# An encoder layer with expert retrieval on one core: 32 bytes of filler, VectorE's dot products first in the slot, and late attention at six pairs per four heads

## The chip, the cores and the metric

The kernel runs on one core of one Trainium2 chip, with float32 data throughout. Its time is the device time of one execution in microseconds; the number that counts is the median of several runs.

## The reference, cut to what matters

One layer over 1024 tokens of width 1024. Every projection, softmax and sum below is computed:

```python
xn = rms_norm(h, norm_mix)
y_r = retention_branch(...); y_s = sgu_branch(...); y_a = window_attention(...)
merged = sigmoid(gate_r) * (y_r @ w_proj_ret) + sigmoid(gate_s) * (y_s @ w_proj_sgu) + sigmoid(gate_a) * (y_a @ w_proj_att)
h = h + merged @ w_out
# PEER: 8 heads choose 16 of 128*128 experts each, per token
gate = softmax(top_s)                      # scores of the 16 chosen
act = gelu(einsum('thkd,td->thk', u_tab[eid], xt))
h = h + einsum('thk,thkd->td', gate * act, v_tab[eid])
h = h + sigmoid(rms_norm(h, norm_ple) @ ple_gate) * (p @ ple_proj)
```

Each token uses 128 experts, each a row of 1024 numbers of u and 1024 of v, 8 KB together. Of 1024 tokens that is 1.07 GB, gathered by index.

## The kernel before, in words

Three stages run one after the other. The first (keys_stage) makes keys, values and states of all eight tiles of 128 tokens, the second (branches_stage) the branches of tiles 0 to 4, and the third (late_stage, TensorE begins it at 458 us) all the rest. It works in **slots**. From slot 34 on (plan.first) a slot holds one **pair**: two expert rows for each token of a tile. There are 512 pairs, 64 for a tile, eight for one of the eight heads of a tile.

For a row, GpSimd issues an indirect DMA into one of eleven row buffers (l_rows, L1425), after the row that was there has been weighed. VectorE multiplies its u half with the token and sums (dot, L2157). ScalarE makes gelu, weight and, for rows that TensorE adds up, a diagonal matrix (weights, L1873, L1877, L1881). The v half is added by VectorE (weigh, L2167, l_acc or l_merged) or by TensorE through the diagonal (weigh, L1641). TENSOR_ROWS divides rows between the two: 4, 5 or 6 of each eight go to TensorE.

Beside the pairs runs everything that prepares later tiles: a planner (class Plan) gives each **job** a slot. Jobs are projections (gate, proj, query and more, whose weights come through a ring of four 1 MB chunks, all_ring and l_ring), transposes, score products, and for tiles 5 to 7 their retention (rq to ryt) and attention (aq to ayt). Tiles are worked in GROUPS (0, 1), (2, 3, 4), (5, 6, 7); group 2 has its gates and merges behind the attention. The order of the work is written out by hand, once per engine, as a loop over slots:

- TensorE, slot s: weigh of pair s - 1 (counted in slots), then the second halves of jobs begun earlier, then the jobs of slot s.
- ScalarE, slot s: its part of the jobs of slot s - 1, exponentials and norms that fall on s, the search's small steps, then weights of the pair of s.
- VectorE, slot s (L2185 to L2218): order.turn, rotations, squares and gates of tiles 5 to 7, scale, normalise, its part of the jobs of slot s - 1 (merge L1975, add_input L1988, mask_scores L2073, scale_values L2092, reciprocal_rms L2098 and more), the two dots of the pair of s, weigh of pair s - 1, finish at a tile's end, output, and the search for coming heads.
- SP loads the ring, scores, inputs and masks, keyed to slots too; ScalarE stores a few tiles.

Late attention (place_attended, L970) works four heads at a time: asc makes the scores of two heads, twice, mask_scores evacuates them and takes the maximum, attention_exponentials (L1794) follows two slots after the second asc, apt transposes the probabilities of two heads, keep_probs (L1801, L1810) copies them in the slot after, apv multiplies with the values, scale_values divides by the sum. All four heads share one buffer of scores (sc) and all pairs of heads share one of turned probabilities (pt), so keep_probs waits for the apv before it:

```python
before = divmod(job.i * (AH // 2) + job.n - 1, AH // 2)
act.wait_ge(pb_done, plan.of["apv", before[0], before[1]].pb[0] + 1)
```

In build_program small constants stand in SBUF ahead of all_ring, all_xt and the tensors of the stages. Their places follow from their order and sizes, each rounded up to 32 B. ident (512 B a partition), eps, col_ple, iota16, col_ret, sink and decays (160 B) take 864 B from address 8320, so that all_ring begins at 9184, all_xt at 25568, and behind them l_rows at 37856 and l_ring at 127968. The first two stages put a col_mix of 32 B at 37856 and the rest of theirs behind it.

The planner's other numbers that the change touches follow from the attention's slots: earliest (L990) for vs, us and yst of group 2, and rate[2] (L1034), which spreads group 2's work over the slots from the last aqt to ends[2].

Of the kernel before, what the change touches and what calls it, by code (L numbers as in the profile page):

```python
# [17 lines left out]
F32 = mybir.dt.float32  # L18
# [5 lines left out]
P = 128  # L24
# [776 lines left out]
def on_tensor(r):  # L801

    return r % 8 in TENSOR_ROWS[r // NSEL] and r != T * NSEL - 1
# [11 lines left out]
class Plan:  # L815
# [154 lines left out]
    def place_attended(self):  # L970

        at = self.of["pgate", PLE_TILES[0][-1], 1].slot + 2
        for i in range(len(BESIDE)):
            job = self.of["aq", i]
            job.head, job.slot = at, at + 1
            at += 3
        base = self.of["aq", 0].slot + 7
        for u in range(2 * len(BESIDE)):
            i, w = u // 2, u % 2 * 2
            if w == 0:  # L980
                self.of["aqt", i].slot = base - 2
            for k, (score, turn, value) in enumerate(((0, 5, 7), (2, 6, 8))):
                self.of["asc", i, w + k].slot = base + score
                self.of["apt", i, w + k].slot = base + turn
                self.of["apv", i, w + k].slot = base + value
            if w:
                self.of["ayt", i].slot = base + 10
            base += 5

    def earliest(self, job):  # L990

# [98 lines left out]
def late_stage(nc, A, R, X):  # L1090
# [3 lines left out]
    with ExitStack() as ctx:  # L1094
# [116 lines left out]
        def pair_of(s):  # L1211

            g = s - plan.first
            return g if 0 <= g < PAIRS else None
# [710 lines left out]
        def _(dve):  # L1925
# [18 lines left out]
            def normalise(g, i):  # L1944

                k = number(g, i)
                dve.wait_ge(std_ready, k + 1)
                order(dve.reciprocal(mv[:, i, 3:4], mv[:, i, 2:3]))
                order(dve.tensor_scalar(vg(i), vg(i), mv[:, i, 0:1], mv[:, i, 3:4], ALU.subtract, ALU.mult))
                dve.wait_ge(ln_in, (g + 1) * 32)  # L1950
                order(tt(vg(i), vg(i), ln_g, ALU.mult))
                tt(vg(i), vg(i), ln_b, ALU.add).then_inc(vn_ready, 1)
                dve.wait_ge(vn_ready, k + 1)
# [36 lines left out]
            def scale(g, i):  # L1990

                k = sum(len(group) for group in GROUPS[:g]) + i
                dve.wait_ge(rms_ready, k + 1)
                order(dve.reciprocal(rms[:, 2:3], rms[:, 1:2]))
                dve.wait_ge(gain_in, 16 if g < 2 else 32)
                dve.scalar_tensor_tensor(out=scaled(g, i), in0=summed(g, i), scalar=rms[:, 2:3], in1=gain[:], op0=ALU.mult, op1=ALU.mult).then_inc(xs_ready, 1)
                dve.wait_ge(xs_ready, k + 1)
# [38 lines left out]
            def gate_retained(i):  # L2036
                y = kept(i)
                dve.wait_ge(ret_rooted, i + 1)
                order(dve.reciprocal(r_rms[:, RH:2 * RH], r_rms[:, RH:2 * RH]))
                freed_pa(dve, plan.of["rg", i].pa[0])  # L2040
                order(tt(by_4(tb), by_4(silu(i)), wide(r_rms[:, RH:2 * RH], RD), ALU.mult))
                tt(y, y, tb, ALU.mult).then_inc(ret_ready, 1)
                dve.wait_ge(ret_ready, i + 1)
# [6 lines left out]
            def square_query(i):  # L2050
                freed_pa(dve, plan.of["aq", i].pa[0])
                order(tt(tb, qa(i), qa(i), ALU.mult))
                dve.tensor_reduce(a_rms[:, i, 0:AH], by_8(tb), AX.X, ALU.add).then_inc(att_squared, 1)
                dve.wait_ge(att_squared, i + 1)

            def rotate_attention(i):

                def finish(ins):
                    ins.then_inc(qa_ready, 1)
                    dve.wait_ge(qa_ready, i + 1)  # L2060

                dve.wait_ge(att_rooted, i + 1)
                order(dve.reciprocal(a_rms[:, i, AH:2 * AH], a_rms[:, i, AH:2 * AH]))
                order(tt(by_8(qa(i)), by_8(qa(i)), wide(a_rms[:, i, AH:2 * AH], AD), ALU.mult))
                order(tt(by_8(qa(i)), by_8(qa(i)), over(a_gain[:], AH), ALU.mult))
                rotate(order, dve, qa(i), qa(i), spins[:, i, 0:AD // 2], spins[:, i, AD // 2:NA], spun, AH, AD // 2, finish)
# [83 lines left out]
            def dot(r):  # L2150

                t, n = r // NSEL, r % TOPK
                if r % NSEL == 0 and K0 <= t < last[0]:
                    dve.wait_ge(xn_in[t % 2], t // 2 * 16)
                dve.wait_ge(row_in[r % SLOTS], (r // SLOTS + 1) * 16)
                u = rows[:, r % SLOTS, 0:D]
                dve.scalar_tensor_tensor(out=u, in0=u, scalar=1.0, in1=xn_of(t), op0=ALU.mult, op1=ALU.mult,  # L2157
                                         accum_out=dots[:, n:n + 1]).then_inc(dot_done, 1)
# [11 lines left out]
            def finish(t):  # L2170

                dve.wait_ge(acc_done, n_dve((t + 1) * NSEL))
                dve.wait_ge(acc2_done, n_pe((t + 1) * NSEL))
                tt(sum_of(t), sum_of(t), acc2[:], ALU.add).then_inc(h2_ready, 1)  # L2174
                dve.wait_ge(h2_ready, t + 1)
# [8 lines left out]
                    scales_at[plan.of["out", g, 1, i].slot + (3 if g else 2 + 2 * i)].append((g, i))  # L2184
            for s in range(plan.n_slots):  # L2185
                order.turn()
                if s in spins_at:
                    rotate_attention(spins_at[s])
                if s in squares_at:
                    square_query(squares_at[s])  # L2190
                if s in gates_at:
                    gate_retained(gates_at[s])
                for g, i in scales_at[s]:
                    scale(g, i)
                for g, i in normed_at[s]:
                    normalise(g, i)
                for job in plan.at[s - 1] if s else ():
                    if job.kind in programs:
                        programs[job.kind](job)
                if pair_of(s) is not None:  # L2200
                    dot(2 * pair_of(s))
                    dot(2 * pair_of(s) + 1)
                g = pair_of(s - 1)
                if g is not None:
                    for r in (2 * g, 2 * g + 1):
                        if not on_tensor(r):
                            weigh(r)
                if g is not None and (2 * g + 2) % NSEL == 0:
                    finish(2 * g // NSEL)
                for t in range(T):  # L2210
                    for half in range(2):
                        if s == plan.of["pgate", t, half].slot + 2:
                            output(t, half)
                for q, part in plan.parts[s]:
                    if part < 2:
                        search_keys(q, part)
                    else:
                        (search_pairs, choose)[part - 2](q)  # L2218
# [7 lines left out]
def build_program(nc, A, X=None):  # L2226
    if X is None:
        X = {n: nc.dram_tensor(f"kept_{n}", s, F32).ap() for n, s in SPILLS.items()}
    with ExitStack() as ctx:
        R = {"semaphores": Semaphores()}  # L2230
        for n, s, d in (("ident", [P, P], F32), ("eps", [P, 1], F32), ("col_ple", [P, DC], F32), ("iota16", [P, TOPK], F32),
                        ("col_ret", [P, RH], F32), ("sink", [P, AH], F32), ("decays", [P, 40], F32)):
            R[n] = ctx.enter_context(nc.sbuf_tensor("all_" + n, s, d))
        R["ring"] = ctx.enter_context(nc.sbuf_tensor("all_ring", [P, 2, CHUNK], F32))
        R["xt"] = ctx.enter_context(nc.sbuf_tensor("all_xt", [P, max(len(group) for group in GROUPS), D], F32))
        with ExitStack() as mixers:
            for n, s in (("col_mix", [P, DC]), ("decay_mask", [P, RH, P]), ("state_f", [P, T + 1, RW]), ("state_b", [P, T + 1, RW]), ("ka_t", [P, T + 2, P]), ("va", [P, T + 2, AKW]),
                         ("w_branches", [P, DC, KEPT * HB])):
                R[n] = mixers.enter_context(nc.sbuf_tensor("mix_" + n, s, F32))
            keys_stage(nc, A, R, X)  # L2240
            R["semaphores"].clear(nc)
            branches_stage(nc, A, R, X)
            R["semaphores"].clear(nc)
        late_stage(nc, A, R, X)
# [87 lines left out]
```

## Time and profile before

| | us |
|---|---|
| median of 3 runs | 3707.91 (3706.53 to 3715.52) |
| the profiled execution's own time | 3710.65 |
| its span, first to last instruction | 3708.9 |
| TensorE / VectorE / ScalarE / GpSimd busy | 3067.4 / 2667.3 / 1392.0 / 1177.5 |
| mean granted TensorE clock | 0.92 |
| bytes moved by DMA | 1288.92 MB, of which 1073.81 by GpSimd's queue |

Busy time counts compute alone. "DMA share" in a table of stretches is the busy share of the 16 DMA engines; packets overlap a little, so it can be above 1. A wait names the engine and line that waited, then what released it. A packet of the queue is one descriptor; the row loads have 128 of 8 KB and 16 short completions each.

### The profile page before, as it was taken

What the parts mean: (1) busy time and instruction counts of PE and PEld (TensorE: products, weight loads), DVE (VectorE), ACT (ScalarE), POOL (GpSimd) and SP (SyncE); (2) the same over time, 40 slices, a digit from 0 to 9 for tenths busy, and PEclk for the clock granted to TensorE, in tenths of its full rate; (3) what the DMA queues carried; (4) which work ended last, traced back from release to release, by engine and by line L of the source; (5) the groups of instructions that cost most, each with busy time, mean ns of one, the idle gap of its engine ahead of it and who ended that gap; (6) DMA issues with size and microseconds to landing.
All of it is one profiled execution on the core that took longest, in us unless ns stands there. A gap on an engine that the chain in (4) does not pass through costs nothing. (4 is left out here: it accounts for less than half of the span.)

```text
span 3708.9 us, 30990 instructions
## 1 busy us (share of the span) xinstructions
PE 3067.4 (83%) x7876; PEld 1410.0 (38%) x7876; DVE 2667.3 (72%) x5261; ACT 1392.0 (38%) x3615; POOL 1177.5 (32%) x1092
## 2 busy tenths in 40 slices
PE   7989899889988897797898988887786677777666
PEld 4545544434433343333443333343232222223222
DVE  4456511678877877888787887877778778778874
ACT  3223211334433433545453443433453344334332
POOL 0000000233433343232243433433445444444442
PEclk9999799989999998898899999999898998889988
DMA  4331144899999999998899999999999999999995
GB/s 158 103 116 42 41 179 162 325 418 419 418 386 378 419 420 418 381 408 316 317 392 418 419 419 419 419 418 417 396 361 416 420 418 419 419 419 410 419 419 240
DMA packets 210625, 1288.92 MB, mean 348 GB/s; under 512 B 24864, under 2 KB 38048, under 8 KB 63904
## 3 DMA queue, kind: packets, MB, share of 16 engines
q0 software_dynamic: 147456, 1073.81, 70.7%
q1 hardware_dynamic: 57680, 202.86, 14.3%
q10 hardware_dynamic: 5328, 10.49, 0.7%
q8 instruction: 55, 0.90, 0.1%
q14 instruction: 106, 0.87, 0.1%
HBM read 1257.31 MB, written 29.75 MB: 347 GB/s over the span
## 5 line engine op out<-in xcount | busy, mean ns | idle before, releaser
L1641 PE MATMUL l_acc<-l_rows,l_diag 128*128 128x512 f32 x2620 | 1407.9, 677 | 558.9 <-ACT l_diag L1881 552.5
L1425 POOL DMA_INDIRECT l_rows<-in_peer_uv,l_at x1024 | 1163.1, 1136 | 1817.7 <-DVE l_acc L2167 1053.8
L1641 PEld LDWEIGHTS l_acc<-l_rows,l_diag 128*128 128x128 f32 x2620 | 527.9, 212 | 1348.6 <-ACT l_diag L1881 798.8
L2157 DVE SCALAR_TENSOR_TENSOR l_rows<-l_rows,l_xn 128x1024 f32<-128x1024 f32 x640 | 766.0, 1223 | 212.0 <-DMA l_rows<-in_peer_uv,l_at 177.0
L2157 DVE SCALAR_TENSOR_TENSOR l_rows<-l_rows,all_xt 128x1024 f32<-128x1024 f32 x384 | 461.5, 1224 | 165.3 <-DMA l_rows<-in_peer_uv,l_at 136.6
L1873 ACT ACTIVATE l_dots<-l_dots 128x2 f32<-128x2 f32 x512 | 104.1, 203 | 1180.2 <-DVE l_rows L2157 1178.5
L2167 DVE SCALAR_TENSOR_TENSOR l_acc<-l_rows,l_wts,l_acc 128x1024 f32<-128x1024 f32 x272 | 349.0, 1283 | 15.6 <-ACT l_wts L1877 15.6
L1877 ACT ACTIVATE l_wts<-l_dots,l_gates 128x1 f32<-128x1 f32 x1024 | 293.6, 287 | 16.8
L1881 ACT ACTIVATE l_diag<-all_ident,l_wts 128x128 f32<-128x128 f32 x655 | 263.0, 402 | 23.1 <-PE l_acc L1641 1.8
L1418 POOL CAST l_at<-l_expert 128x16 uint32<-128x16 f32 x64 | 14.2, 222 | 667.4 <-DVE l_expert L2143 667.2
L1873 ACT ACT_TABLE_LOAD x139 | 178.3, 1283 | 69.5 <-DVE l_rows L2157 68.2
L1456 PE MATMUL l_pa<-all_ring,all_xt 128*128 128x512 f32 x384 | 178.9, 610 | 4.4 <-PEq L77 4.4
L1465 PE MATMUL l_pa<-l_ring,all_xt 128*128 128x512 f32 x392 | 178.5, 598 | 0.0
L1456 PE MATMUL l_pa<-l_ring,all_xt 128*128 128x512 f32 x360 | 163.6, 597 | 1.3 <-ACT all_xt L1726 1.3
L1465 PE MATMUL l_pa<-all_ring,all_xt 128*128 128x512 f32 x352 | 159.3, 595 | 0.0
L2167 DVE SCALAR_TENSOR_TENSOR l_merged<-l_rows,l_wts,l_merged 128x1024 f32<-128x1024 f32 x97 | 124.3, 1281 | 7.9 <-ACT l_wts L1877 7.8
L1456 PEld LDWEIGHTS l_pa<-all_ring,all_xt 128*128 128x128 f32 x384 | 75.4, 199 | 98.3 <-issue 98.3
L1465 PEld LDWEIGHTS l_pa<-l_ring,all_xt 128*128 128x128 f32 x392 | 75.8, 193 | 96.5 <-issue 96.5
L1695 ACT ACTIVATE l_sgk<-l_pa 128x512 f32<-128x512 f32 x48 | 28.7, 597 | 197.1 <-PE l_pa L1465 197.0
L1975 DVE TENSOR_TENSOR l_sgk<-l_pb,l_sgk 128x512 f32<-128x512 f32 x32 | 22.1, 691 | 110.3 <-PE l_pb L123 107.4
L1465 PEld LDWEIGHTS l_pa<-all_ring,all_xt 128*128 128x128 f32 x352 | 67.6, 192 | 85.8 <-issue 85.8
L1456 PEld LDWEIGHTS l_pa<-l_ring,all_xt 128*128 128x128 f32 x360 | 68.1, 193 | 84.3 <-issue 82.5
(351 smaller groups left out, 3426.1 us busy)
## 6 DMA issues: line engine op xcount, KB each, us to landing
l_ring<-in_w_late SPq DMA_DIRECT2D x58, 1024.0 KB
all_ring<-in_w_late SPq DMA_DIRECT2D x56, 1024.0 KB
l_rows<-in_peer_uv,l_at POOLq DMA_INDIRECT x1024
kept_s<-l_yt ACTq DMA_DIRECT2D x31, 256.0 KB
l_s_in<-kept_s SPq DMA_DIRECT2D x62, 128.0 KB
mix_w_branches<-in_w_branches_kept SPq DMA_DIRECT2D x8, 768.0 KB, 4.3
all_xt<-kept_xnt SPq DMA_DIRECT2D x9, 512.0 KB, 21.7
k_x<-in_x SPq DMA_DIRECT2D x8, 512.0 KB, 5.5
```

The costliest lines, as they stand in the source:

```text
L1418: pool.tensor_copy(at[:, c % 2, :], expert[:, c % 3, :]).then_inc(at_ready, 1)
L1425: pool.indirect_dma_start(out=rows[:, r % SLOTS, :], out_offset=None, in_=A["peer_uv"], in_offset=bass.IndirectOffsetOnAxis(ap=at[:, c % 2 ...
L1456: pe.matmul(out, x[:, c * P:(c + 1) * P], wide_chunk(job.chunk, c), start=(c == 0), stop=False)
L1465: last = pe.matmul(out, x[:, c * P:(c + 1) * P], wide_chunk(job.chunk, c), start=False, stop=(c == DC - 1))
L1641: ins = pe.matmul(acc2[:, hs], diag[n_pe(r) % DIAGS][:], rows[:, r % SLOTS, D + half * HB:D + (half + 1) * HB], start=first, stop=last)
L1695: act.activation(sg(job.i), pa[job.pa[0] % 2][:], ACT.Sigmoid).then_inc(pa_free[job.pa[0] % 2], 1)
L1873: act.activation(dots[:, n:n + 2], dots[:, n:n + 2], ACT.Gelu).then_inc(act_done, 1)
L1877: ins = act.mul(wts[:, m:m + 1], dots[:, m:m + 1], gates[:, c % 3, m:m + 1])
L1881: act.mul(diag[n_pe(r) % DIAGS][:], R["ident"][:], wts[:, m:m + 1]).then_inc(diag_ready, 1)
L1975: evacuate(n, tt(part_sum, pb[n % 4][:], sg(job.i), ALU.mult))
L2157: dve.scalar_tensor_tensor(out=u, in0=u, scalar=1.0, in1=xn_of(t), op0=ALU.mult, op1=ALU.mult, accum_out=dots[:, n:n + 1]).then_inc(dot_do ...
L2167: dve.scalar_tensor_tensor(out=sum_of(t), in0=rows[:, r % SLOTS, D:2 * D], scalar=wts[:, n:n + 1], in1=sum_of(t), op0=ALU.mult, op1=ALU.ad ...
```

## The change

- In build_program a tensor all_even of 8 numbers (32 B a partition) is put ahead of all_ring. Nothing reads or writes it.
- In VectorE's loop the two dots of a slot stand right behind order.turn, ahead of the slot's jobs.
- In place_attended four heads take six slots in place of five: scores at 0 and 3 (before 0 and 2), transposes at 6 and 8 (5 and 6), values at 8 and 10 (7 and 8), the transpose of the finished tile at 12 (10).

```diff
--- before.py
+++ after.py
@@ -979,13 +979,13 @@
             i, w = u // 2, u % 2 * 2
             if w == 0:
                 self.of["aqt", i].slot = base - 2
-            for k, (score, turn, value) in enumerate(((0, 5, 7), (2, 6, 8))):
+            for k, (score, turn, value) in enumerate(((0, 6, 8), (3, 8, 10))):
                 self.of["asc", i, w + k].slot = base + score
                 self.of["apt", i, w + k].slot = base + turn
                 self.of["apv", i, w + k].slot = base + value
             if w:
-                self.of["ayt", i].slot = base + 10
-            base += 5
+                self.of["ayt", i].slot = base + 12
+            base += 6
 
     def earliest(self, job):
 
@@ -2184,6 +2184,9 @@
                     scales_at[plan.of["out", g, 1, i].slot + (3 if g else 2 + 2 * i)].append((g, i))
             for s in range(plan.n_slots):
                 order.turn()
+                if pair_of(s) is not None:
+                    dot(2 * pair_of(s))
+                    dot(2 * pair_of(s) + 1)
                 if s in spins_at:
                     rotate_attention(spins_at[s])
                 if s in squares_at:
@@ -2197,9 +2200,6 @@
                 for job in plan.at[s - 1] if s else ():
                     if job.kind in programs:
                         programs[job.kind](job)
-                if pair_of(s) is not None:
-                    dot(2 * pair_of(s))
-                    dot(2 * pair_of(s) + 1)
                 g = pair_of(s - 1)
                 if g is not None:
                     for r in (2 * g, 2 * g + 1):
@@ -2231,6 +2231,7 @@
         for n, s, d in (("ident", [P, P], F32), ("eps", [P, 1], F32), ("col_ple", [P, DC], F32), ("iota16", [P, TOPK], F32),
                         ("col_ret", [P, RH], F32), ("sink", [P, AH], F32), ("decays", [P, 40], F32)):
             R[n] = ctx.enter_context(nc.sbuf_tensor("all_" + n, s, d))
+        R["even"] = ctx.enter_context(nc.sbuf_tensor("all_even", [P, 8], F32))
         R["ring"] = ctx.enter_context(nc.sbuf_tensor("all_ring", [P, 2, CHUNK], F32))
         R["xt"] = ctx.enter_context(nc.sbuf_tensor("all_xt", [P, max(len(group) for group in GROUPS), D], F32))
         with ExitStack() as mixers:
```

## Rows read from the trace of the kernel before

**Rows 1.** The profile's page: busy shares, and GB/s moved in 40 slices

```profile
PE 3067.4 (83%) x7876; PEld 1410.0 (38%) x7876; DVE 2667.3 (72%) x5261; ACT 1392.0 (38%) x3615; POOL 1177.5 (32%) x1092
GB/s 158 103 116 42 41 179 162 325 418 419 418 386 378 419 420 418 381 408 316 317 392 418 419 419 419 419 418 417 396 361 416 420 418 419 419 419 410 419 419 240
```

**Rows 2.** The page's chain of work that ended last

```profile
DMA 8%; PE 1%; issue 1%; DVE 1%; ACT 0%; POOL 0%; DVEq 0%; POOLq 0%
```

**Rows 3.** Stretches: us; busy PE, PEld, DVE, ACT, POOL; clock, DMA share, GB/s

```profile
680.00:1060.00 380.00, 340.28 (x829) 152.88 (x830) 297.15 (x559) 156.29 (x375) 133.22 (x124) 0.94 1.01 417
1060.00:1200.00 140.00, 123.04 (x288) 54.57 (x287) 104.25 (x203) 48.35 (x125) 42.71 (x42) 0.94 0.94 373
1200.00:1540.00 340.00, 290.90 (x825) 139.56 (x826) 269.70 (x503) 139.57 (x360) 119.09 (x112) 0.94 1.02 418
1540.00:1600.00 60.00, 46.42 (x125) 21.37 (x123) 49.42 (x99) 25.67 (x65) 19.41 (x19) 0.86 0.92 351
1660.00:1880.00 220.00, 180.35 (x558) 90.24 (x557) 177.50 (x358) 113.66 (x281) 67.64 (x66) 0.91 0.84 321
1880.00:2640.00 760.00, 650.34 (x1561) 287.52 (x1559) 602.57 (x1185) 300.53 (x817) 299.59 (x277) 0.93 1.01 418
2640.00:2780.00 140.00, 122.06 (x272) 52.65 (x272) 105.99 (x214) 74.72 (x182) 61.00 (x53) 0.92 0.92 366
2780.00:3660.00 880.00, 607.94 (x1132) 235.75 (x1132) 701.15 (x1421) 326.81 (x1007) 399.20 (x366) 0.88 1.01 417
```

**Rows 4.** Waits in 1660 to 1880 us: who for whom, total, times, longest

```profile
DVE l_yt L2073 <- PE l_pb L1589: 13.2, 5, 8.3
DVE l_ht L2092 <- PE l_pb L1606: 13.2, 4, 5.0
DVE l_bn L1939 <- ACT l_merged L1672: 5.8, 1, 5.8
ACT l_gain L1810 <- PE l_pb L1606: 31.0, 5, 9.7
PE l_acc L1641 <- ACT l_diag L1881: 36.7, 18, 7.6
POOL l_rows L1425 <- DVE l_acc L2167: 115.9, 23, 11.9
```

**Rows 5.** VectorE's waits in 1060 to 1200, 1540 to 1600, 2640 to 2780

```profile
DVE l_sgk L1975 <- PE l_pb L123: 13.6, 2, 7.7
DVE l_merged L1988 <- PE l_pb L1465: 11.5, 3, 6.5
...
DVE l_yt L2048 <- PE l_pb L1551: 6.7, 1, 6.7
DVE l_prms L2098 <- ACT l_prms L1830: 1.5, 1, 1.5
...
DVE l_prms L2098 <- ACT l_prms L1830: 19.4, 3, 7.3
```

**Rows 6.** VectorE's waits for rows in 2050 to 2300 us

```profile
DVE l_rows L2157 <- DMA l_rows<-in_peer_uv,l_at: 30.2, 24, 3.8
```

**Rows 7.** Groups by line: the dot products of 640 rows

```profile
L2157 DVE SCALAR_TENSOR_TENSOR l_rows<-l_rows,l_xn 128x1024 f32<-128x1024 f32 x640 | 766.0, 1223 | 212.0 <-DMA l_rows<-in_peer_uv,l_at 177.0
```

**Rows 8.** DMA in 11.5 to 17.5, 527.2 to 529.8, 2900 to 3100 us

```profile
DMA packets 1215, 2.46 MB, mean 409 GB/s; under 512 B 16, under 2 KB 16, under 8 KB 1215
q1 hardware_dynamic: 1215, 2.46, 105.1%
...
DMA packets 151, 1.11 MB, mean 425 GB/s; under 512 B 16, under 2 KB 16, under 8 KB 16
q1 hardware_dynamic: 151, 1.11, 100.6%
...
DMA packets 12352, 83.80 MB, mean 419 GB/s; under 512 B 1373, under 2 KB 2013, under 8 KB 2269
```

**Rows 9.** Timeline of VectorE at the first rows: start, us, what

```profile
680.14 1.23 DVE L2157 SCALAR_TENSOR_TENSOR l_rows<-l_rows,l_xn 128x1024 f32<-128x1024 f32 x1 [3.79 <-DMA l_rows<-in_peer_uv,l_at]
```

## The prediction

> **What bounds the kernel now.** First the page's slices [rows 1]: from the ninth on, the sixteen DMA engines move 416 to 420 GB/s in most slices, while TensorE is busy 83% and VectorE 72% of the span. The chain that ended last [rows 2] names the landing of expert rows with 8%, everything else with 1% or less. The reader should see a transfer-bound kernel with an even ceiling, so that the question is where it falls below the ceiling. The table of stretches [rows 3] answers: 417 to 418 GB/s in the four long ones, less in four short ones. With 419 as the ceiling (the mean of the fullest stretch, [rows 8]), the transfer time lost is W x (419 - rate) / 419: 140 x 46/419 = 15 us in 1060 to 1200, 60 x 68/419 = 10 us in 1540 to 1600, 220 x 98/419 = 52 us in 1660 to 1880 (the late attention, pairs 183 to 213), 140 x 53/419 = 18 us in 2640 to 2780 (the gates of tiles 2 to 4). Sum: 95 us. As the bytes do not change, the change can win only from these 95 us, or by raising the ceiling.
>
> Why the ceiling is missed in the attention stands in its waits [rows 4]. GpSimd, which issues the rows, waits 116 us for VectorE to free a row: transfers run dry because rows are held, not because issuing is slow. VectorE is busy 177.5 of 220 us [rows 3]; of its 42.5 us idle, 26.4 are waits for TensorE's attention scores (L2073) and values (L2092). TensorE waits 36.7 us for the diagonals of ScalarE, and ScalarE waits 31.0 us at L1810, five times and up to 9.7 us, for TensorE's values (L1606). That is a ring: the probabilities of the second pair of heads are copied in the same slot in which TensorE makes the values of the first, ScalarE's row weights stand behind that copy, and TensorE's values stand behind the weights of the slot before.
>
> **The change part by part.** *The filler.* Tensors are laid out in order at multiples of 32 B, so 32 B more move the first ring from 9184 (17 x 512 + 480) to 9216 (18 x 512), and the rows from 37856 to 37888 (74 x 512); both now begin 224 B past a multiple of 256. The tensors of the first two stages, aligned now behind their 32 B col_mix, go 32 B off. The trace has both kinds [rows 8]. Loads of weights in 2 KB packets to an aligned tile (11.5 to 17.5 us) keep the engines full at 409 GB/s, 16 x 2048 / 409 = 80.1 ns a packet. Ring loads in 8 KB packets, misaligned (527.2 to 529.8 us), reach 425 GB/s with their completions, 308.4 ns. The difference, 228.3 ns for 6144 B, is 26.9 B/ns, and leaves 80.1 - 76.1 = 4 ns fixed for the aligned packet and 308.4 - 304.5 = 4 ns for the misaligned one. No room is left for a cost of the start address, so I take 0. Bounds: a misaligned row packet could be what separates rows (419) from that ring load (425): (425 - 419) / 425 = 1.4% of the 2360 us in the four full stretches [rows 3], 33 us gained; nothing excludes the same in the other sense for the tiles that go off, but there the slices show 41 to 179 GB/s [rows 1], so it is hidden under TensorE, with 2 us as bound if the saturated 6 us load lost a third.
>
> The row speaks against any gain here. The Trainium skill (DMA: Bandwidth & Descriptors, section How a descriptor splits into AXI transactions) speaks for one: a transfer that begins off a 256 B boundary also pays for the bytes below its start, here 7 beats of 32 B on 256, or 2.7%. As an estimate by that page 2.7% of about 2850 us would be 76 us and the sum would end near 3590; by that rule the misaligned load could not have reached 425 with its completions, and the trace does not agree.
>
> *Dot products first.* In each slot VectorE now does the two dots (2 x 1.22 us, [rows 7]) before the rotations, scalings and evacuations of the slot before; then the weighing, as now. Nothing is added and no DMA is issued by the moved code; SP's and GpSimd's lists keep their order, and only the semaphores of VectorE's jobs rise later, those of the dots earlier. The length of the cycle changes. Now dots(s) stand behind jobs(s-1), which need TensorE's slot s-1, which needs ScalarE's weights(s-2), which need dots(s-2): one pass of the ring serves two slots. Afterwards only dots(s+1) stand behind it, so that it serves three. Each wait of VectorE for a job is covered by 2.45 us more work.
> - 1060 to 1200: waits of 13.6 and 11.5 us for TensorE in 5 pieces [rows 5]; 5 x 2.45 = 12 us covered, 8 taken, since TensorE is busy 123 of 140 and 15 is all that can be won.
> - 1540 to 1600: one wait of 6.7 and one of 1.5 us; 2.45 + 1.5 = 4 taken.
> - 2640 to 2780: VectorE waits three times, 19.4 us, for ScalarE's root of the tile (L2098); 3 x 2.45 = 7 covered, 5 taken, because ScalarE's own chain of that job is as long as before.
>
> In the full stretches the cost is a later job: dots wait for rows there, 30.2 us in 24 pieces in 250 us [rows 6], 1.3 us each, and each job is now behind that and 2.45 us of dots. Cover: rows are asked for 5 pairs ahead, TensorE is idle 110 of 760 us in 1880 to 2640. I put 5 us for it all, with bounds of 0 and the rival below. In the opening the first dots wait 3.8 us for their landing [rows 9] before jobs that then are later by that, on a VectorE with nothing urgent: 0, at most 4.
>
> *Six pairs per four heads.* Attention takes 35 slots to its last turn now (base to base + 35), 42 then; scores at 0 and 3 of 6 in place of 0 and 2 of 5, transposes 6 and 8, values 8 and 10. The second copy of probabilities (slot 9) meets values made in slot 8, so the 31.0 us of L1810 lose their reason, and with them most of the diagonals' 36.7. What then bounds is VectorE's own work: 177.5 busy and some 9 us of gaps between its instructions (42.5 less 26.4, 5.8 for L1939 and a little) give 187 in place of 220. The seven slots more are ordinary ones, where VectorE idles 157 of 760 us [rows 3], about 1.2 us a pair: up to 8 us further relief, of which the longer chain of exponentials (now behind the later masks) takes part. Transfers alone need 220 x 321/419 = 169. I take a gain of 30, bounds 10 (only L1810's share that falls on a row release) and 52. Group 2 behind it gets 125 slots for what had 129, TensorE's work there 3% denser: 20 us of work into 110 us of idle time, 0, and its last score comes 3 slots later, long before the tiles need it. What is late next is VectorE itself.
>
> Sum: 30 + 8 + 4 + 5 - 5 - 0 = 42 us off. The profiled execution took 3710.65 us (span 3708.9), so it would be 3669; it stands 2.7 us above the median of 3707.91, for which the forecast is 3666.
>
> **The rivals.** (1) *The start address counts after all*, worth 33 us by rows: 3666 - 33 = 3633, and down to 3590 by the rule named above. Against it the packet times [rows 8]; for it only that rows run at 419 and not 425, which their issue by GpSimd can explain. Chance 0.10. (2) *The wait moves and little comes of it*: with VectorE free in the attention, ScalarE's exponentials and TensorE, busy 180 of 220 us, keep the rows held; a gain of 10 less 5: 3703. Chance 0.15. (3) *Slower: jobs behind the row wait.* In 1880 to 2640 each of group 2's 27 evacuations (18 merges, 6 outputs, 3 mixings) is later by the dots and, at worst, the longest row wait, 2.45 + 3.8 = 6.25 us; if TensorE stood still each time, 27 x 6.25 = 169 us against its 110 us idle: 59 lost, 42 won, 3725. It decides from 110/27 = 4.1 us a job on. For it: TensorE at 86% is the next engine to be full. Against: four buffers of PSUM and jobs placed two or more slots apart. Chance 0.14. (4) That the change does not do what it says touches the filler alone, whose effect I count as nothing; the two reorderings change instructions directly.
>
> **How the numbers follow.** A measurement of this kernel can tell about 0.3%, 11 us, from no change. The forecast's case has 0.61, rival 1 0.10, together 0.71 faster; rival 2 lies around the edge, 0.01 of it beyond: faster 0.72, same 0.14, slower 0.14. The likeliest case alone spans 3629 (79 of the 95 us) to 3696. The range takes in all 95 us (3613) and reaches up past the middle of no change to 3710; left out are the far part of rival 1 (0.04) and rival 3 with its neighbours (0.14).
>
> **What would show it.** Right: about 390 GB/s or more from 1660 to 1920, L1810's waits for TensorE gone, L2073's and L2092's under 10 us together, GpSimd's wait for L2167 there halved; L2098's waits shorter by 2 us each. 419 GB/s where it was full shows the filler idle, 425 rival 1. Wrong: TensorE waiting for pb buffers or for L1975 in 1880 to 2640, and below 415 GB/s there (rival 3); the attention still at 330 GB/s with ScalarE waiting at L1798 (rival 2).

## The result, and the profile after

The changed kernel takes 3619.57 us (median of 4 runs, 3616.38 to 3624.38), the kernel before 3709.52 us in the same comparison (4 runs, 3706.53 to 3715.52). The ratio is 0.9757, 95% interval 0.974 to 0.9774. So 90 us are gone, 2.4%, more than twice the 42 of the forecast; the time is inside the range, near its lower end. The profiled execution has a span of 3614.6 us.

The page of the changed kernel, its busy line, its GB/s in 40 slices and its chain, against [rows 1, 2]:

```profile
PE 3027.8 (84%) x7876; PEld 1398.3 (39%) x7876; DVE 2668.0 (74%) x5261; ACT 1389.0 (38%) x3612; POOL 1207.9 (33%) x1092
GB/s 154 97 129 43 27 172 169 287 425 426 426 426 426 424 425 407 410 405 351 397 400 426 426 427 426 427 425 425 420 409 424 427 422 421 422 419 401 427 424 240
DMA 3%; PE 1%; issue 1%; DVE 0%; ACT 0%; POOL 0%; DVEq 0%; POOLq 0%
```

Two things are to be seen. The dips are shallower: the attention's slices stood at 316 and 317, now the lowest is 351, and those at 386, 378 and 381 are gone. And the ceiling itself has risen: full slices stood at 418 to 420 GB/s and now stand at 425 to 427. Counts and busy times are almost those of before: nothing became cheaper on an engine.

The stretches of the changed kernel (us; busy PE, PEld, DVE, ACT, POOL; granted clock, DMA share, GB/s), against [rows 3]:

```profile
680.00:1060.00 380.00, 348.69 (x864) 156.74 (x865) 305.43 (x578) 162.73 (x390) 139.96 (x129) 0.96 1.01 425
1060.00:1200.00 140.00, 123.21 (x294) 55.30 (x293) 117.77 (x215) 59.16 (x145) 55.09 (x48) 0.94 1.01 426
1200.00:1540.00 340.00, 289.26 (x842) 142.24 (x843) 276.16 (x534) 136.40 (x362) 118.44 (x111) 0.92 1.00 414
1540.00:1600.00 60.00, 55.68 (x125) 24.08 (x124) 51.81 (x98) 25.51 (x63) 27.61 (x22) 0.95 1.00 408
1660.00:1880.00 220.00, 193.95 (x627) 97.68 (x628) 198.92 (x410) 116.79 (x307) 89.81 (x80) 0.92 0.95 380
1900.00:2600.00 700.00, 604.39 (x1455) 268.64 (x1454) 560.26 (x1104) 286.68 (x772) 288.75 (x261) 0.95 1.01 426
2640.00:2780.00 140.00, 114.78 (x247) 47.49 (x246) 118.80 (x248) 66.43 (x184) 63.89 (x59) 0.94 1.01 415
2780.00:3500.00 720.00, 499.12 (x948) 193.73 (x947) 583.11 (x1203) 272.03 (x831) 329.14 (x303) 0.89 1.01 421
```

Stretches are cut by the clock, not by work, so a row of after holds somewhat later work than its row of before; the steps are read in the rates, not in the busy times. 680 to 1060 and 1900 to 2600 were full before (417 and, within [rows 3], 418) and are full now, at 425 and 426. Of the four short stretches one is full (426), two are nearly so (408 and 415) and the attention is mended in part (380). Two full stretches have lost a little of their fullness: 414 in 1200 to 1540 and 421 in 2780 to 3500, under a ceiling of 426.

The waits of the changed kernel in 1660 to 1880 us (who for whom: us, times, longest), against [rows 4]:

```profile
DVE l_yt L2073 <- PE l_pb L1589: 8.5, 4, 3.3
DVE l_ht L2092 <- PE l_pb L1606: 2.2, 1, 2.2
ACT l_gain L1810 <- PE l_pb L1597: 28.6, 9, 6.7
PE l_acc L1641 <- ACT l_diag L1881: 27.6, 9, 6.7
POOL l_rows L1425 <- DVE l_acc L2167: 110.6, 26, 8.8
```

VectorE's waits for TensorE's scores and values went from 26.4 to 10.7 us. ScalarE's wait at L1810 for the values (L1606) is gone, but ScalarE now stands 28.6 us at the same line for the transposes (L1597; 6.5 us before). GpSimd's wait for VectorE to free a row is nearly what it was, while it issues 74 rows in that time and not 62: 115.9 / 62 = 1.9 us a row before, 110.6 / 74 = 1.5 now.

VectorE's waits of the changed kernel in 1060 to 1200, in 2640 to 2780 and in 2050 to 2300 us, against [rows 5, 6]:

```profile
DVE l_merged L1988 <- PE l_pb L1465: 7.5, 4, 4.1
DVE l_sgk L1975 <- PE l_pb L123: 3.3, 1, 3.3
...
DVE l_prms L2098 <- ACT l_prms L1830: 3.3, 1, 3.3
...
DVE l_rows L2157 <- DMA l_rows<-in_peer_uv,l_at: 26.2, 18, 3.1
```

### The profile page after: what moved, and what is told of

Same layout as the page of the kernel before. It is cut to its first block and busy times, and to the rows that moved or that the text cites. A ratio compares the mean times of both kernels' runs of the same rounds, so it can differ in the third digit from the quotient of the medians.

```text
span 3614.6 us, 30882 instructions
## 1 busy us (share of the span) xinstructions
PE 3027.8 (84%) x7876; PEld 1398.3 (39%) x7876; DVE 2668.0 (74%) x5261; ACT 1389.0 (38%) x3612; POOL 1207.9 (33%) x1092
## 5 line engine op out<-in xcount | busy, mean ns | idle before, releaser
L1641 PE MATMUL l_acc<-l_rows,l_diag 128*128 128x512 f32 x2620 | 1383.4, 668 | 501.2 <-ACT l_diag L1881 494.6
L1425 POOL DMA_INDIRECT l_rows<-in_peer_uv,l_at x1024 | 1191.7, 1164 | 1694.6 <-DVE l_acc L2167 952.3
L2167 DVE SCALAR_TENSOR_TENSOR l_acc<-l_rows,l_wts,l_acc 128x1024 f32<-128x1024 f32 x272 | 349.3, 1284 | 7.2 <-ACT l_wts L1877 3.8
L2167 DVE SCALAR_TENSOR_TENSOR l_merged<-l_rows,l_wts,l_merged 128x1024 f32<-128x1024 f32 x97 | 124.3, 1282 | 4.2 <-ACT l_wts L1877 4.0
L522 PE MATMUL b_p<-mix_w_branches,b_xnt 128*128 128x512 f32 x192 | 92.1, 632 | 0.0
```

Of the source, the lines that this page charges most:

```text
L522: last = pe.matmul(out[:], x[:, c, :], R["w_branches"][:, c, column:column + HB], start=(c == 0), stop=(c == DC - 1))
L1425: pool.indirect_dma_start(out=rows[:, r % SLOTS, :], out_offset=None, in_=A["peer_uv"], in_offset=bass.IndirectOffsetOnAxis(ap=at[:, c % 2 ...
L1641: ins = pe.matmul(acc2[:, hs], diag[n_pe(r) % DIAGS][:], rows[:, r % SLOTS, D + half * HB:D + (half + 1) * HB], start=first, stop=last)
L2167: dve.scalar_tensor_tensor(out=sum_of(t), in0=rows[:, r % SLOTS, D:2 * D], scalar=wts[:, n:n + 1], in1=sum_of(t), op0=ALU.mult, op1=ALU.ad ...
```

## The experiments

The forecast said that the filler does nothing and that the two reorderings give 42 us. So the three parts were first run one by one, then the filler was taken from the whole. Times below are medians. The kernel before was measured beside each group of experiments: 3710.13 us beside the first four (11 runs), 3710.7 beside the three starts and the first of "both aligned", 3709.61 beside the last three.

**The filler alone.**

```diff
+        R["even"] = ctx.enter_context(nc.sbuf_tensor("all_even", [P, 8], F32))
         R["ring"] = ctx.enter_context(nc.sbuf_tensor("all_ring", [P, 2, CHUNK], F32))
```

> The 32 B filler alone on the kernel before. Theory A (start address): misaligned packets cost some 4 to 6 ns each once transfers have been continuous for 10 to 15 us, so the ceiling goes from 419 to 426 GB/s for the whole row stage, 1.6% of about 2850 us: 46 us less, 3664, with the slow attention stretch still there at about 325 GB/s. Rival O (order): the higher rate in the changed kernel came with the dots' new place, which spreads VectorE's accesses; then the filler alone is worth under 8 us and the full stretches stay at 419.

3675.91 us (3670.4 to 3680.29), ratio 0.9905 [0.9888, 0.9921]: 34 us gained by 32 B that hold nothing. Two of its stretches, columns as above:

```profile
1660.00:1880.00 220.00, 178.65 (x574) 90.35 (x575) 175.97 (x358) 113.97 (x281) 68.50 (x66) 0.92 0.84 322
1900.00:2600.00 700.00, 611.53 (x1460) 270.76 (x1459) 561.56 (x1093) 281.76 (x763) 289.19 (x260) 0.94 1.01 426
```

The attention stays at its 322, but what was full at 419 is now full at 426. By this one run the step "so I take 0" has fallen. The stretch from 680 to 1060, full before, gained nothing by itself: it moved 417 GB/s with and without the filler.

**The dot products first, alone.**

```diff
                 order.turn()
+                if pair_of(s) is not None:
+                    dot(2 * pair_of(s))
+                    dot(2 * pair_of(s) + 1)
...
-                if pair_of(s) is not None:
-                    dot(2 * pair_of(s))
-                    dot(2 * pair_of(s) + 1)
```

> Only the dots moved ahead, no filler, attention at five slots. Theory A: ceiling stays at 419 GB/s; the short stretches recover 25 to 35 of the 95 us lost, 3675 to 3685, and most of the attention's loss (ScalarE at L1810) remains. Rival O: ceiling 424 or more, 3640 or less.

3670.8 us (3668.04 to 3673.93), ratio 0.9892 [0.9875, 0.9909]: 39 us. Its stretches, and its waits in 1660 to 1880 us:

```profile
1060.00:1200.00 140.00, 124.65 (x297) 55.95 (x295) 115.37 (x212) 55.64 (x138) 52.68 (x46) 0.96 1.01 419
1200.00:1540.00 340.00, 289.38 (x840) 141.62 (x840) 270.79 (x516) 132.95 (x352) 118.61 (x109) 0.92 1.01 411
1660.00:1880.00 220.00, 192.84 (x629) 98.45 (x628) 193.30 (x387) 117.05 (x300) 82.33 (x76) 0.95 0.91 358
...
ACT l_gain L1810 <- PE l_pb L1606: 41.0, 6, 11.2
PE l_acc L1641 <- ACT l_diag L1881: 19.0, 12, 4.7
DVE l_ht L2092 <- PE l_pb L1606: 6.8, 2, 4.0
DVE l_yt L2073 <- PE l_pb L1589: 2.8, 3, 1.7
```

Here is the row that corrects the picture of the attention. ScalarE's wait at L1810 for the values grew, from 31.0 to 41.0 us, and yet TensorE waits only 19.0 us for the diagonals (36.7 before) and the rate rose from 321 to 358. What fell is VectorE's waiting for scores and values, from 26.4 to 9.6 us. That wait of ScalarE was long and cost little.

**Six pairs per four heads, alone.**

```diff
-            for k, (score, turn, value) in enumerate(((0, 5, 7), (2, 6, 8))):
+            for k, (score, turn, value) in enumerate(((0, 6, 8), (3, 8, 10))):
...
-                self.of["ayt", i].slot = base + 10
-            base += 5
+                self.of["ayt", i].slot = base + 12
+            base += 6
```

> Only the six slots per four heads. If ScalarE's wait at L1810 for TensorE's values is what holds the attention, it disappears and 20 to 30 us come off, 3680 to 3690, with the stretches before 1660 us as in the kernel before. If VectorE's waits for TensorE hold it (then it is the dots' place that matters), under 10 us.

3701.45 us (3690.91 to 3706.33, 8 runs), ratio 0.9972 [0.996, 0.9983]: 9 us. Its attention, and its waits in 1660 to 1880 us:

```profile
1660.00:1880.00 220.00, 176.27 (x528) 85.71 (x528) 176.29 (x356) 105.57 (x264) 65.90 (x67) 0.88 0.87 334
...
PE l_acc L1641 <- ACT l_diag L1881: 41.4, 16, 8.3
DVE l_yt L2073 <- PE l_pb L1589: 27.5, 5, 8.7
ACT l_gain L1810 <- PE l_pb L1597: 25.6, 7, 6.3
```

The wait for the values is gone as foretold, and TensorE waits for the diagonals more than before (41.4 against 36.7 us), VectorE for TensorE 27.5 at L2073 alone (13.2 before). The spacing breaks the link that the forecast named, and the wait moves on, as rival 2 had it. A likely reason, not tested by itself, is that VectorE still stands in its jobs before it comes to the dots.

**Both reorderings, no filler.**

```diff
-        R["even"] = ctx.enter_context(nc.sbuf_tensor("all_even", [P, 8], F32))
```

> The changed kernel without its filler. Theory A: 46 us slower than the changed kernel, 3665, ceiling 419 GB/s. Rival O: within 8 us of 3620. If the parts add, this gain and that of the filler alone sum to 90 us.

3661.95 us (3660.69 to 3666.58), ratio 0.9867 [0.9851, 0.9884]: 48 us, which is 39 + 9 of the two alone. Its stretches:

```profile
1060.00:1200.00 140.00, 128.03 (x306) 57.61 (x305) 117.65 (x222) 56.87 (x142) 51.76 (x46) 0.96 1.01 419
1200.00:1540.00 340.00, 288.54 (x823) 140.44 (x822) 266.20 (x507) 132.13 (x346) 122.31 (x112) 0.91 1.01 411
1540.00:1600.00 60.00, 47.40 (x125) 21.76 (x124) 53.66 (x108) 25.73 (x66) 23.08 (x19) 0.91 0.96 375
1660.00:1880.00 220.00, 185.30 (x604) 92.90 (x603) 200.23 (x400) 119.58 (x311) 86.59 (x77) 0.92 0.94 374
1900.00:2600.00 700.00, 601.29 (x1439) 265.15 (x1437) 551.76 (x1076) 279.24 (x748) 283.82 (x255) 0.95 1.01 419
2640.00:2780.00 140.00, 118.66 (x271) 50.37 (x270) 117.43 (x234) 74.14 (x197) 63.41 (x57) 0.96 1.00 407
2780.00:3500.00 720.00, 492.28 (x935) 192.13 (x933) 573.41 (x1176) 267.99 (x817) 311.77 (x298) 0.89 1.01 413
```

This kernel is the one that the forecast of 3666 describes. Without the filler the ceiling is back at 419.

**Which boundary, and which rule.** Three kernels differ from the changed one in the filler's size alone, so that rings and rows begin on a multiple of 256 but not of 512, 32 B past a multiple of 256, and 128 B past one (before: 224 B past). The filler has 288, 64 and 160 B for that; each cut is against the changed kernel.

```diff
-        R["even"] = ctx.enter_context(nc.sbuf_tensor("all_even", [P, 8], F32))
+        R["even"] = ctx.enter_context(nc.sbuf_tensor("all_even", [P, 72], F32))
```

> The changed kernel with 288 B of filler, so that rows and weights begin at an odd multiple of 256 B. Theory A1: the cost comes from a start off a 256 B boundary; then this is as fast as the changed kernel, 3620, with row stretches at 426 GB/s. Rival A2: 512 B is the unit; then as without filler, 3662, 419 GB/s.

3619.76 us (3617.5 to 3625.85), ratio 0.9765 [0.9748, 0.9782]: the changed kernel's time. A multiple of 256 is enough.

```diff
-        R["even"] = ctx.enter_context(nc.sbuf_tensor("all_even", [P, 8], F32))
+        R["even"] = ctx.enter_context(nc.sbuf_tensor("all_even", [P, 16], F32))
```

> The changed kernel with 64 B of filler: rows and weights begin 32 B past a multiple of 512. If bytes below the start are paid for (the rule of beats), 1 beat of 32 B in 256 here in place of 7: 0.4% of 2850 us, at most 11 us over 3620, 3626 to 3631. If it is one more transaction for a packet whatever the offset, the same as without filler: 3660, 419 GB/s.

3661.51 us (3657.61 to 3664.06), ratio 0.9875 [0.9858, 0.9891]: the time without a filler (3661.95). 32 B past a boundary cost as much as 224.

```diff
-        R["even"] = ctx.enter_context(nc.sbuf_tensor("all_even", [P, 8], F32))
+        R["even"] = ctx.enter_context(nc.sbuf_tensor("all_even", [P, 40], F32))
```

> The changed kernel with 160 B of filler: rows and weights begin 128 B past a multiple of 256. By beats below the start 4 of the 7, 24 us over 3620: 3644, about 422 GB/s. By one more transaction for a packet: 3660, 419 GB/s.

3652.12 us (3650.06 to 3655.36), ratio 0.985 [0.9834, 0.9866]: it costs 32 of the 42 us. DMA in 2000 to 2200 us of the kernel before and of these three, in this order (before, 256, 32, 128):

```profile
DMA packets 12006, 83.81 MB, mean 419 GB/s; under 512 B 1331, under 2 KB 1843, under 8 KB 1843
...
DMA packets 12328, 85.29 MB, mean 426 GB/s; under 512 B 1360, under 2 KB 2000, under 8 KB 2000
...
DMA packets 12009, 83.85 MB, mean 419 GB/s; under 512 B 1329, under 2 KB 1841, under 8 KB 1841
...
DMA packets 12049, 84.14 MB, mean 421 GB/s; under 512 B 1334, under 2 KB 1846, under 8 KB 1846
```

Single packets say the same. Counted from the packet records of the expert rows (8 KB each) in 2800 to 3200 us:

```
kernel              start past 256   mean ns   at 309 ns   at 313 ns
before              224 B            315.3      8%         50%
both reorderings    224 B            317.4     23%         42%
start 32 past        32 B            317.0     20%         44%
start 128 past      128 B            315.9     44%          7%
start 256             0 B            312.3     98%          0%
changed kernel        0 B            311.8     99%          0%
```

A packet to an unaligned start takes 313 ns most often, in place of 309, whether it is 32 or 224 B past; in the mean it is 5 to 6 ns more (317.0 and 317.4 against 311.8 and 312.3). At 128 B 44% of the packets stay at 309 and 53% lie between 311 and 321 ns, and the cost in time is three quarters of the others'; no theory here foretold that, and it stays open.

**What else goes unaligned, and where the gain sits.** The filler puts the tensors of the first two stages 32 B off. This kernel aligns them as well:

```diff
-            for n, s in (("col_mix", [P, DC]), ("decay_mask", [P, RH, P]), ...
-                         ("w_branches", [P, DC, KEPT * HB])):
+            for n, s in (("decay_mask", [P, RH, P]), ...
+                         ("w_branches", [P, DC, KEPT * HB]), ("col_mix", [P, DC]), ("pad", [P, 120])):
```

> The changed kernel with the first two stages' tensors at multiples of 512 B as well (their 32 B col_mix goes to the end, with 480 B behind it). The 2 KB weight packets of the first 20 us, 88 ns in the changed kernel, should be 84 again as in the kernel before. Theory: the first key products start 0.5 us earlier, everything else there is hidden under TensorE; 0 to 2 us off 3620. Rival: the early stages pay in every transfer, 3 to 6 us off.

3613.81 us (3613.44 to 3620.3), ratio 0.975 [0.9732, 0.9767], 6 us under the changed kernel with intervals that overlap. The stretches showed no place for a gain, so it was measured a second time, together with a kernel in which only the rows and what stands behind them are aligned: no filler ahead of the rings, 32 B ahead of the rows in its place.

```diff
-        R["even"] = ctx.enter_context(nc.sbuf_tensor("all_even", [P, 8], F32))
...
+        pad = sb("pad", [P, 8])
         rows = sb("rows", [P, SLOTS, 2 * D])
```

> The changed kernel without its filler ahead of the rings; in its place 32 B stand directly ahead of the expert rows. So rows and the late rings begin on a multiple of 256 B, the first rings, the x tiles and the late tensors of the first stages stay as they were before the change (the tensors of the first two stages aligned, the first rings 224 B past a multiple). Theory (the cost of an unaligned start falls on the row packets, because they keep the transfers full for long): all of the filler's gain is back, 3613 to 3622 us, rows at 425 to 427 GB/s from 1900 to 2600 us and 8 KB packets of 309 ns. Rival (the rings' alignment carries part of it): 3630 to 3650 us.

3620.36 us (3615.94 to 3621.57), ratio 0.9765 [0.9749, 0.9782]: the changed kernel's time. Rows at a multiple of 256, with the two ring chunks (l_ring) behind them, are all of the gain; the first two ring chunks (all_ring) and the x tiles count for nothing that can be measured. Rows and l_ring were not taken apart.

> The kernel of e8_both_aligned a second time, in more rounds: everything that is loaded begins on a multiple of 256 B, the tensors of the first stages too. It was 5.8 us under the changed kernel there, with intervals that overlapped. Theory (early transfers are hidden under TensorE, so nothing but a little of the first weight load can be won): within 2 us of the rows-only kernel of the same call. Rival (the first load's slower packets are on the path): 3 to 8 us under it.

3620.92 us (3618.52 to 3625.42), ratio 0.9767 [0.975, 0.9785]. The 6 us were not there a second time, on another chip and beside the rows-only kernel: nothing that repeats is gained by aligning the early stages.

The rows-only kernel gives the cleanest look at the first load of weights (2 KB packets), which it has aligned and the changed kernel 32 B off. Stretches of 2 us of that load, first of the changed kernel, then of rows only:

```profile
11.50:13.50 2.00, 0.85 (x4) 0.88 (x5) 0.92 (x2) 0.00 (x0) 0.00 (x0) 1.00 1.05 410
13.50:15.50 2.00, 1.09 (x6) 0.69 (x4) 0.82 (x1) 0.00 (x0) 0.00 (x0) 1.00 1.04 392
15.50:17.50 2.00, 0.80 (x1) 0.50 (x2) 0.92 (x4) 0.90 (x1) 0.00 (x0) 1.00 1.05 389
```

```profile
11.50:13.50 2.00, 0.83 (x4) 0.86 (x5) 0.92 (x2) 0.00 (x0) 0.00 (x0) 1.00 1.05 410
13.50:15.50 2.00, 1.11 (x6) 0.71 (x4) 0.80 (x1) 0.00 (x0) 0.00 (x0) 1.00 1.05 408
15.50:17.50 2.00, 0.87 (x1) 0.50 (x2) 0.94 (x4) 0.88 (x1) 0.00 (x0) 1.00 1.05 408
```

Both start at 410. Only after about 2 us does the unaligned load fall to 392 and 389. The forecast's witness for "no cost" was a ring load, of which this is the course in the kernel before:

```profile
526.00:528.00 2.00, 2.00 (x6) 0.85 (x5) 0.00 (x0) 0.00 (x0) 0.00 (x0) 1.00 0.77 299
528.00:530.00 2.00, 2.00 (x6) 0.95 (x5) 0.69 (x1) 0.00 (x0) 0.00 (x0) 1.00 0.99 418
530.00:532.00 2.00, 2.00 (x6) 0.85 (x5) 0.22 (x1) 0.00 (x0) 0.00 (x0) 1.00 0.67 283
```

It was full for some 4 us (527 to 531), longer than those 2 us, so the first load alone doesn't explain why it showed no cost. The 8 KB packets themselves do. In the kernel before, where all of them go to unaligned starts, 98% of the row packets from 680 to 684 us took 309 ns, 69% from 684 to 688 and 5% from 688 to 692, with transfers at 0.96 or more of full from 674 us on. With 8 KB packets the cost came some ten microseconds into full transfers, and this ring load, whose packets took 309 ns from 528 to its end, was over by then. Why the cost comes late at all, and later for 8 KB than for 2 KB, no run here shows.

**The spacing once more, with the filler and the early dots.**

```diff
-            for k, (score, turn, value) in enumerate(((0, 6, 8), (3, 8, 10))):
+            for k, (score, turn, value) in enumerate(((0, 5, 7), (2, 6, 8))):
...
-                self.of["ayt", i].slot = base + 12
-            base += 6
+                self.of["ayt", i].slot = base + 10
+            base += 5
```

> The changed kernel with five pairs per four heads again: filler and early dots stay. Without the filler the spacing was worth 3670.8 - 3661.95 = 8.9 us on top of the early dots. Theory (the parts are linked only by the share of the time in which transfers are full): the spacing is worth a little more with faster transfers, 9 to 16 us, so 3629 to 3636 us, with the attention from 1660 to 1880 us near 363 to 370 GB/s. Rival (the spacing's worth is already in the early dots, and 8.9 was noise): within 4 us of the changed kernel, 3620 to 3624 us.

3631.89 us (3624.87 to 3634.16), ratio 0.9797 [0.9781, 0.9814]; attention and gates:

```profile
1660.00:1880.00 220.00, 196.05 (x646) 99.95 (x645) 194.76 (x402) 114.67 (x294) 86.65 (x78) 0.97 0.92 369
2640.00:2780.00 140.00, 115.17 (x240) 48.01 (x238) 115.38 (x242) 64.48 (x174) 71.37 (x60) 0.90 0.99 398
```

So the spacing is worth 12 us on top of the two others. With all runs side by side, each part alone and on top of others:

```
part       alone   on top of
filler     34.2    42.4 (both reorderings)
dots       39.3    39.5 (spacing), 44.0 (filler)
spacing     8.7     8.9 (dots), 12.3 (filler and dots)
```

The 82 us of the parts alone make 90 together. Stretches cut by the clock hold different work in each kernel, so here is the same split by work. Counted from the issue times of the rows (L1425): when the first is issued, how long the kernel takes from the issue of one pair to that of another, and what is left behind the last pair, in us of the profiled executions.

```
pairs           before  filler   dots  spacing  both, no filler  changed
first issue      668.1   668.3   663.9   667.6        672.4       667.3
0 to 96          609.6   609.6   600.7   606.2        600.3       590.6
96 to 160        431.8   426.1   423.3   432.4        424.5       417.4
160 to 256       589.1   580.4   570.8   582.4        560.1       554.5
256 to 320       370.9   364.9   371.6   371.6        369.3       363.0
320 to 511       989.0   971.9   987.6   984.4        986.4       970.2
to the end        50.6    52.9    51.5    52.3         51.9        51.7
```

The filler alone gains nothing in pairs 0 to 96, and 9.7 us there on top of the reorderings (600.3 to 590.6). That is where its 34 us become 42: faster transfers pay only where nothing else holds the rows back, and the early dots have taken other waits out of those pairs. The first issue moves by up to 8.5 us between these kernels (663.9 to 672.4), by no part in particular; that was not run down.

## Why the prediction was wrong, and where it was right

**The filler, the step that failed.** The forecast took two packet times, aligned 2 KB at 80.1 ns and misaligned 8 KB at 308.4 ns, solved them for 4 ns fixed in both kinds, and wrote "No room is left for a cost of the start address, so I take 0". The runs show 34 us alone and 42 on top. Three faults lie in the step. First, the working could not have found a cost: with one rate drawn through two packet times, the time left over is the same 4 ns at both by construction, and any price of an unaligned start would have gone into the rate of 26.9 B/ns. Second, the misaligned figure came from a burst of 2.6 us, before such a load shows its cost, as the packet times above say. And third, the row that spoke against it stood in the same group [rows 8]: the rows' own 419 over 200 us, which was set aside as "their issue by GpSimd". With the filler the same gathers run at 426. Rival 1 had 33 us, from a ceiling of 425 in place of 419 over the four full stretches, and that is the 34 of the filler alone, in part by luck: one of the four, 680 to 1060, gained nothing. On top of the reorderings it was 42, and the difference sits in pairs 0 to 96. From both reorderings to the changed kernel the rate rises by 7 GB/s in 680 to 1060, in 1060 to 1200 and in 1900 to 2600 (the last alone is 700 x 7/419 = 12 us), by 8 in 2780 to 3500, by 6 in the attention and by 3 in 1200 to 1540.

**What the Trainium skill's rule was right and wrong in.** The forecast said of the Trainium skill (DMA: Bandwidth & Descriptors, section How a descriptor splits into AXI transactions) that the trace does not agree. In direction it agrees: a start off a 256 B boundary costs, and one at a multiple of 256 doesn't. In size it does not. Paying for the bytes below the start would make 224 B cost 7 beats and 32 B one. (The section words this for bytes that are fetched; the filler moves the written side, in SBUF, so the runs speak of that side alone.) As an estimate by that page of the Trainium skill these are 76 us, as the forecast had it, and a seventh of it, 11 us; measured were 42 and 42. What fits rows of both sizes is a fixed price of a packet: 16 x 2048 B at 410 and 389 GB/s are 79.9 and 84.2 ns, 4.3 ns more; 8 KB packets go from 309 to 313 ns at their most common, 4 ns more, and by 5 to 6 ns in the mean. That this is one more transaction per packet is an inference; no run isolates it, and 128 B, with its spread, doesn't quite follow it.

**The reorderings, right in sum.** Their sum was 42, measured 48 (3666 forecast, 3661.95 measured with both and no filler; the profiled executions are only 44 apart, 3710.65 and 3666.58, the latter being the slowest of its four). Taken apart as W x (rate gained) / 419, from [rows 3] to that kernel's stretches:

```
stretch        GB/s        gives   forecast
1060 to 1200   373 to 419   15.4      8
1540 to 1600   351 to 375    3.4      4
1660 to 1880   321 to 374   27.8     30
2640 to 2780   366 to 407   13.7      5
1200 to 1540   418 to 411   -5.7     } -5
2780 to 3500   417 to 413   -6.9     }
sum                         47.7     42
```

The rates flatter the short stretches and blame the long ones behind them. By work, from the table of pairs, both reorderings gain 9.3 us in pairs 0 to 96, 7.3 in 96 to 160, 29.0 in 160 to 256, 1.6 in 256 to 320 and 2.6 in 320 to 511, and the start and the end lose 4.3 and 1.3: together 44, the distance of the two profiled executions.

- *1060 to 1200.* The forecast took 8 us. All 15 that could be won came by the clock, but pairs 64 to 80 take 10 us less (112.0 to 102.0) and pairs 80 to 96 then 10.6 more (96.3 to 106.9). Transfers are full in those (418 GB/s from 1166 to 1266 us), so they carry bytes there that the kernel before had moved earlier. What is kept up to pair 96 is 9.3 us, part of it from 680 to 1060, where the forecast had none.
- *2640 to 2780.* L2098 runs three times, and in the changed kernel two of these come before 2640 us, so the one wait of 3.3 us above is not the whole. All three, in 2560 to 2780, for the kernel before, dots alone, both without filler, and the changed kernel:

```profile
DVE l_prms L2098 <- ACT l_prms L1830: 19.4, 3, 7.3
DVE l_prms L2098 <- ACT l_prms L1830: 12.5, 3, 5.0
DVE l_prms L2098 <- ACT l_prms L1830: 6.8, 3, 3.6
DVE l_prms L2098 <- ACT l_prms L1830: 8.0, 3, 3.6
```

The dots alone shorten each by 2.3 us, as forecast; the rest came with the spacing, by a way that was not run down. In time little of it is kept, 2.6 us from pair 320 to the last.
- *The attention's 30 us* was right in size and wrong in cause, so its size is luck. (It lies at pairs 149 to 179; the 183 to 213 of the forecast are slots.) It was put on the spacing, by way of the wait at L1810. The dots alone give 220 x 37/419 = 19 us there with that wait longer than before; the spacing alone 220 x 13/419 = 7 with that wait gone. By work it is the same: 18, 7 and 29 us for dots, spacing and both in pairs 160 to 256. That the wait that decided is VectorE's own, at L2073 and L2092, fits the dots (26.4 to 9.6 us) but is not shown: with the spacing alone these two waits grew to 31.2 us and the rate still rose, to 334. "L1810's waits for TensorE gone" was a wrong sign too: they now go to L1597. Two more signs were narrowly missed, 387 GB/s from 1660 to 1920 where 390 was asked, and 10.7 us at L2073 and L2092 where it was under 10.
- *GpSimd's wait for L2167 halved* did not come (115.9 to 110.6). There are eleven row buffers whatever the speed; the wait per row is what fell, from 1.9 to 1.5 us.
- *Later jobs, -5.* In 1880 to 2640, where the forecast looked, there is no loss: 418 GB/s with both reorderings, and waits for rows in 2050 to 2300 are 26.2 us in the changed kernel, 30.2 before. Of rival 3's signs one wait of TensorE for L1975 is seen, 3.4 us. By rates 13 us are lost in 1200 to 1540 and in 2780 to 3500, but by work no block of pairs in the table is slower than before, so much of that can be the same bytes moved at another time. One new dip is plain, 345 and 394 GB/s from 1440 to 1480 with both reorderings (416 and 419 before); its cause was not run down, and VectorE in 1380 to 1460 of the changed kernel waits for little but rows.

## What to carry to other kernels

Where transfers set the time, put the tiles that most bytes go to at a multiple of 256 B in their partition, and look at where the allocation really lands: 864 B of small constants ahead of the big tiles, where 896 would have done, cost this kernel 42 of 3662 us, 1.1%. A price read from a burst of 2.6 us says nothing about a stream of milliseconds, and two points give a rate and a fixed part but can't also show a third cost. Take a rate from the longest full stretch and doubt any explanation that lets it differ from a shorter one. When an engine in a ring of waits is the one that frees buffers, try first in its slot the work on which the others wait; a long wait of another engine (L1810 here) can grow while the kernel gets faster. And compare kernels by the same work as well as by the clock: a wait that has left a window may only have moved ahead of it.

## What the runs showed of the hardware that was not expected

- A start 32 B past a multiple of 256 costs what 224 B past does: 3661.51 and 3661.95 us, 419 GB/s both, against 3619.76 and 426 at a multiple of 256 that is none of 512. 128 B past lies between, 3652.12 us at 420 to 421.
- The cost is 4 to 6 ns a packet at 2 KB and at 8 KB alike, so 5% of a stream of 2 KB packets (410 to 389 GB/s) and 1.6% of one of 8 KB (426 to 419). It comes late: after some 2 us at the full rate with 2 KB packets, and with 8 KB packets between 684 and 692 us, in transfers that were full from 674 us on.
- One kernel, measured on two chips, gave 3613.81 and 3620.92 us, with 3710.7 and 3709.61 for the kernel before beside it: a difference of 0.2% in the median of four or five runs is not yet a result.
